# Another spread of filler matmuls over the heads of the recurrent stage of a decoder-layer kernel

## What is computed

```
# mLSTM: 4 heads, 512 prompt tokens (chunkwise in the reference), 8 samples with a state each
s    = (q k^T) * exp(d_log - m_t);  den = w_inter * (q n) + s.sum(-1)
num  = w_inter * (q C) + s v;       h   = num / max(|den|, exp(-m_t))
C_new = a * C + sum_s w k v^T;      n_new = a * n + sum_s w k
h    = layer-normalised per head, * norm_a_g * sigmoid(a_o)
# merge gates, computed from x alone
gates = sigmoid(einsum('btd,de->bte', x, w_merge))       # (544, 2 * 1024)
```

## The kernel before, in words

| place | c | e3 | e2 | e1 | e0 | g | u1 | u2 | u3 | end |
|---|---|---|---|---|---|---|---|---|---|---|
| steps | 16 | 8 | 4 | 4 | 4 | 4 | 3 | 3 | 2 | 8 |

## Time and profile before

### The profile page before, as it was taken

How to read it: one execution, slowest core, us unless ns; L and a number is a source line. 1 busy time by engine, 2 the same in 40 slices (tenths; PEclk the granted TensorE clock), 3 DMA queues, 4 the chain that set the end, 5 groups by cost and what they waited for, 6 DMA issues and landing times.

```text
span 2187.4 us, 34346 instructions
## 1 busy us (share of the span) xinstructions
PE 2112.9 (97%) x13300; PEld 1868.0 (85%) x13300; DVE 1481.9 (68%) x3063; ACT 986.9 (45%) x1763; POOL 922.1 (42%) x608
## 2 busy tenths in 40 slices
PE   9999999987998998999999999999999999999998
PEld 8898988775565996999999999999998877888886
DVE  4334233346776556487989979876648789888886
ACT  2121332233777431333346676676544455445542
POOL 0000332312110001337877767777765555555530
PEclk9999999997999999999999999999999999999999
DMA  4354343346110543327888899999999999999992
GB/s 148 96 192 116 108 124 102 115 174 164 45 41 1 180 149 113 108 69 230 292 269 298 304 340 319 325 381 403 378 324 404 397 394 377 385 393 393 385 361 84
DMA packets 191242, 518.58 MB, mean 237 GB/s; under 512 B 15796, under 2 KB 85544, under 8 KB 186600
## 3 DMA queue, kind: packets, MB, share of 16 engines
q1 hardware_dynamic: 139656, 330.80, 42.8%
q0 software_dynamic: 50848, 184.53, 22.7%
q10 hardware_dynamic: 576, 1.05, 0.1%
HBM read 446.70 MB, written 73.75 MB: 238 GB/s over the span
## 4 chain that ended last, share of the span: by engine, by line
PE 55%; DVE 3%; DMA 1%; ACT 1%; POOL 0%; issue 0%; DVEq 0%
PE ps_e L2515 23%; PE ps_e L2490 8%; PE ps_e L2485 7%; PE ps_e L2484 7%; PE ps_e L2507 3%; PE ps_e L2539 1%; PE ps_e L2545 1%; PE ps_e L2550 1%; PE ps_e L2546 1%; PE ps_e L2473 1%; DMA v_raw<-in_peer_v 1%; DVE row L2880 1%; DVE one_b L2864 0%; DVE one_a L2864 0%; POOL u_lo L2433 0%
## 5 line engine op out<-in xcount | busy, mean ns | idle before, releaser
L2426 POOL DMA_INDIRECT row<-in_peer_v,sparse_idx x160 | 277.6, 1735 | 209.1 <-DVE y L2888 158.5
L2484 PE MATMUL ps_e<-hTh,u_hi 128*128 128x384 f32 x1024 | 347.1, 339 | 0.0
L2485 PE MATMUL ps_e<-hTl,u_hi 128*128 128x384 f32 x1024 | 346.7, 339 | 0.0
L2433 POOL TENSOR_TENSOR u_lo<-u_raw,u_hi 128x1024 fp32r<-128x1024 f32 x128 | 312.7, 2444 | 66.5 <-ACT u_hi L2590 58.9
L2515 PE MATMUL ps_e<-v_hi,w_hi 128*128 128x512 f32 x768 | 242.4, 397 | 3.2 <-DVE v_lo L2908 3.2
L2515 PE MATMUL ps_e<-v_lo,w_hi 128*128 128x512 f32 x768 | 240.9, 394 | 0.0
L2515 PE MATMUL ps_e<-v_hi,w_lo 128*128 128x512 f32 x768 | 240.6, 394 | 0.0
L2908 DVE TENSOR_TENSOR v_lo<-v_raw,v_hi 128x1024 fp32r<-128x1024 f32 x128 | 158.0, 1237 | 90.1 <-ACT v_hi L2629 89.7
L2490 PE MATMUL ps_e<-hTh,u_lo 128*128 128x384 f32 x1024 | 207.8, 345 | 3.9 <-POOL u_lo L2433 3.9
L2629 ACT CAST v_hi<-v_raw 128x1024 fp32r<-128x1024 f32 x128 | 128.2, 1049 | 156.4 <-DMA v_raw<-in_peer_v 156.4
L2880 DVE CUSTOM_DVE_ANT_0 row<-row,ps_e 128x1024 f32<-128x1024 f32 x150 | 178.8, 1213 | 27.4 <-DMA row<-in_peer_u,sparse_idx 25.4
(11 more groups left out here) (539 smaller groups left out, 4558.7 us busy)
## 6 DMA issues: line engine op xcount, KB each, us to landing
u_raw<-in_peer_uT SPq DMA_DIRECT2D x128, 512.0 KB, 5.8
v_raw<-in_peer_v SPq DMA_DIRECT2D x30, 2048.0 KB, 10.2
hidden_gelu<-gelu_out SPq DMA_DIRECT2D x64, 384.0 KB, 6.4
gate_tables<-g_buf SPq DMA_DIRECT2D x48, 512.0 KB, 9.8
e_gate<-gate_tables SPq DMA_DIRECT2D x31, 768.0 KB, 13.0
gelu_in<-hidden_gelu SPq DMA_DIRECT2D x31, 768.0 KB, 12.9
w_raw<-in_w_tiles SPq DMA_DIRECT2D x45, 512.0 KB, 3.6
gw_raw<-in_merge_tiles SPq DMA_DIRECT2D x16, 512.0 KB, 3.8
```

Of the source, the lines that this page charges most:

```text
L2426: pool.indirect_dma_start(out=row[:, :], out_offset=None, in_=io.peer_u if i < U_END else io.peer_v, in_offset=bass.IndirectOffsetOnAxis(a ...
L2433: pool.tensor_tensor(u_lo[n % UB][:, :, :], u_raw[n % UB][:, :, :], u_hi[:, n % UH, :, :].bitcast(F32), ALU.subtract).then_inc(ul_done, 1)
L2484: pe.matmul(ps[:, n % 2, 0:TD], u_hi[:, n % UH, dc, :], hTh[:, dc, :], start=(dc == 0), stop=False)
L2485: pe.matmul(ps[:, n % 2, 0:TD], u_hi[:, n % UH, dc, :], hTl[:, dc, :], start=False, stop=False)
```

## The change

Before, each place had one number for all heads. After, it has one per head:

```diff
     fill_at, filled = {}, 0
+    spread = {"c": (17, 17, 17, 22), "e3": (8, 8, 8, 12), "e2": (4, 4, 4, 8), "e1": (4, 4, 4, 4), "e0": (4, 4, 4, 4),
+              "g": (4, 4, 4, 3), "u1": (3, 3, 3, 0), "u2": (3, 3, 3, 0), "u3": (2, 2, 2, 0), "end": (8, 8, 8, 0)}
     for key, steps in ([("scan", 24), ("cols", 8)] +
-                       [((h, k), n) for h in range(AH)
-                        for k, n in (("c", 16), ("e3", 8), ("e2", 4), ("e1", 4), ("e0", 4), ("g", 4), ("u1", 3), ("u2", 3),
-                                     ("u3", 2), ("end", 8))]):
+                       [((h, k), spread[k][h]) for h in range(AH)
+                        for k in ("c", "e3", "e2", "e1", "e0", "g", "u1", "u2", "u3", "end")]):
         fill_at[key] = (filled, filled + steps)
         filled += steps
     assert filled == 16 * GT
```

## The result

| | before | after |
|---|---|---|
| median, us | 2195.15 (5 executions, 2194.07 to 2195.67) | 2219.91 (5 executions, 2217.20 to 2226.37) |
| the profiled execution, us | 2189.14 | 2226.37 |
| its span, us | 2187.4 | 2224.7 |
| mean granted clock in it | 0.988 | 0.981 |

The ratio of the medians is 1.0113 (95% interval 1.0098 to 1.0128): 24.8 us slower. That is on the side of the forecast and 2 us beyond the end of its range (2218). In five executions of the same program the granted clock was 0.981, 0.982, 0.984, 0.985 and 0.985, with 2226.4, 2221.4, 2219.9, 2217.5 and 2217.2 us: the time goes with the clock, and the profiled execution is the slowest of the five.

What follows compares the result with a forecast made beforehand. The recurrent stage goes at TensorE's pace, its stalls paid in full. 17.6 + 1.9 - 3.0 = +16.5 us: 2205.6 us from the profiled execution, 2210.8 from the median; range 2205 to 2218.

Steps and rivals of the forecast that it cites:

- The unit ends: Recurrent stage: 22 more filler units end inside a call of fill, each stalling TensorE 0.80 us; +17.6 us.
- ScalarE late: Rival: at seven places in e1 and g ScalarE's copy starts late, 0.5 us more each; +3.6 us, chance 0.08.
- not slower: Rival: the added unit ends cost nothing, something else takes the stalls in; -1.1 us, 2193.2 us, chance 0.05.
- The last head's order: Last head: fillers move ahead of the update products, which then take 5.7 us; VectorE's chain starts 3.5 us later.
- the tail: Stage's end: updates ending 3.5 us later less 1.6 from the early table load; net +1.9 us, between +1.1 and +4.5.
- The next stage: Behind the recurrent stage: wc off the path, pages landing some 8 us behind the opening, not 11.1; -3.0 us.
- its cover: Last head's state store: the whole tail still covers it; otherwise it would hold up SyncE's pages 4 to 7; counted at nothing.
- The early load of -1.6 us: Last head: ScalarE's table load runs ahead of the square root, so a 1.73 us delay shrinks to 0.1.
- The clock: Rival: TensorE's pauses bring one 6.8 us stretch at 1.2 GHz in each head; +13.6 us, 2224.4 us, chance 0.06.

Runs made afterwards that it cites:

- the second profile: The changed kernel measured once more, unaltered, with no 17.1 us clock fall in the heads of its profile: 2223.33 us, ratio 1.0123.
- the split of "c": Kernel before, with 8 of the 16 filler steps in each head's first call moved behind the prompt state's products: 2193.66 us, ratio 0.9988.
- the kernel with the full clock there: Kernel before, fillers in c cut in two around the prompt state's products, last head's 56 steps all ahead of its updates: 2196.94 us, ratio 1.0008.

## Why the prediction was wrong at its end, and right in its main term

**The unit ends: right.** The forecast had 28 places, 22 of them new, at 0.80 us, +17.6. The trace has 28 waits, gaps of 0.87 and 0.20, 12.5 us more idle time and the restart besides. Between the stage's start and the first update of the last head the second profile has 196.5 us and before has 171.35, +25.1; 6.1 of it are the fillers moved ahead and at most 1.7 a fall of 3.4 us at 308.4, which leaves 17.3 to 19.0. (Kernels with 2 to 7 places have such a short fall at that point in some profiles too, so it is not counted to the change.) Between the first updates of heads 0, 1 and 2 that profile has 46.6 and 45.65 us, as forecast (45.5 to 46.7). The shift of one, of two and of three heads give 0.72, 0.64 to 0.74 and 0.79 us a place, the last two from executions at before's clock, and the split of "c" 0.6 by the medians and 0.82 by the traces.

**ScalarE late, and "not slower": both refuted.** No gap in e1 or g is longer than the others, and no place is free.

**The last head's order: mechanism right, size a little small, by the clock.** From the first update product to the end of the last update I had 5.7 us. It is 5.74 in the kernel with the full clock there (470.53 to 476.27), but 6.9 in both profiles of the changed kernel (499.18 to 506.12 in the first), where the clock fell 2.2 and 2.0 us into the updates. From the first update to the transposes of line 831 both take 12.8 us; before it was 15.8 with 6.1 us of fillers in it. So the tail cost 3.1 us instead of 1.9; in the kernel with the full clock in its updates it is 11.6 us, which makes 1.9. The difference of 1.2 us goes with a fall of the clock that the forecast did not have (13.7 us long in both profiles, where before has 6.8 behind its updates). The table load went ahead, as taken from the earlier trace rows, and VectorE's chain to line 948's end took 2.87 us (2.89 forecast).

**The next stage: this step failed.** "So **-3.0 us**, between 0 and -4.7": it was +0.7 and +1.6 in the two profiles, counted from the start of the transposes to the first product on pages (20.8 and 21.8 us, before 20.14); with the last head's order alone it was 0.0. The gain was not there, for two reasons.

The larger part is the pages. wc did leave the path, as forecast, but the pages did not come 8 us behind VectorE's first work: they came 10.7 and 11.4 us behind it (before 11.1), 2.7 and 3.4 late. I had taken the 366 GB/s of the earlier trace rows for them, from a stretch in which wc, pages 4 to 7 and pages 8 to 15 were under way together. With bqT and wc out of the way the span up to the first product on pages moved 219 GB/s (303 before). SyncE's four issues alone ran until 526.43, 4.3 us behind VectorE's first work, and TensorE had its pages 6.4 us after that. So an emptier queue did not bring them sooner. My bound of 0 ("the pages land as late as now") held this part to within 0.3 us, my central value did not.

The smaller part is the barrier, and it was in no bound. From the transposes to VectorE's first work it is 10.1 and 10.4 us, before 9.0: 1.1 and 1.4 more. I had written that without its cover "the state store would hold up SyncE's pages 4 to 7", and then that this "is in the bound of 0"; but SyncE must issue them before the barrier can open, so the delay comes on top of the other terms. The cover did go, and not because the store came late against the tail: bqT and wc now leave ahead of it. The idle time ahead of the barrier went from 1.10 to 2.85 and 3.13 us, and is 3.34, 4.01 and 6.66 in three kernels with the same turn of order. Part of it does not count, since the last transposes pass sooner. With the barrier in it the upper bound should have been about +2. By this step the forecast was 3.7 to 4.6 us low.

The early load of -1.6 us was no gain of its own in the kernel before (0.9996, with an interval of 0.9987 to 1.0006), where the DMA chain would have swallowed it. In the changed kernel VectorE waited 1.75 and 2.0 us longer at the barrier than before, which is more than those 1.6, so it is not shown to have gained anything there either: the path to the barrier ran from the last update (506.12) over the store (506.63) and the page issues (517.17), past the square root and the transposes.

**The clock: a rival with a chance of 0.06 that came true in part.** I priced four falls of 6.8 us, one in each head. It was one of 17.1 us, in four of the five profiles with 16 places or more. Its price from the two profiles of the changed kernel: from the stage's start to the first update of the last head they take 203.8 and 196.5 us, 7.3 apart, and both have the short fall of 3.4 us. I had also put the pauses too close, at one "every 3 to 4 us": in the heads they stand 3.6 to 12.4 us apart without the fall, some 6.6 on average, as seven to a head of 46 us would have told. The row from 540 to 560, on which I rested the low chance, has short pauses at full clock, but it is another stage with other products. The Trainium skill (TensorE: Matmul & The Clock Gate, "A second HAM failure mode: psum-queue depth-cycling") describes micro-idles that make the clock swing; by that rule, which no row of before bore out, the runs agree in kind, with one fall in the heads and not a swinging: in the 84 us ahead of the fall in the profile after, none of TensorE's twelve waits on line 993 was over 0.6 us.

The sum by the second profile, without the long fall: 17.6 + 3.1 + 1.6 = 22.3 us, or 23.7 to the first product on pages (231.04 from the stage's start, before 207.31), as the trace has it with the short fall. Over 2194.8 (before at a clock of 0.988) that is 2217.1 to 2218.5, where the fastest executions of the changed kernel lie (2217.2 to 2217.9); with one fall it is 2224.4 to 2225.8, where its slowest do (2225.3 to 2226.4). Against the forecast of +16.5 the measured +24.8 is 8.3 more: by this sum 4.6 are the next stage, 1.2 the tail, and the other 2.5 or so the fall, which a part of the executions has. Without the fall the sum, 22.3, already stands at the upper end of the 12.7 to 22.3 that I had added up.

**What stays open.** Why one execution has the fall and another has not. A fall of 17.1 us stood in the heads in four of the five profiles with 16 places or more and in none of the nine with fewer (one of 3.4 us stood in head 0's updates when head 0 alone was shifted), so it goes with the pauses; whether their number in a head, their spacing, or the updates behind them decide was not told apart. That executions between 2218 and 2225 us have shorter falls is argued from their clocks alone; they have no profile. The widest spreads, 16.8 us with the shift alone and 14.9 with two heads, are twice the price of one fall, and what those slowest executions have is not shown. Shorter falls, of 3.4 to 13.7 us, stand behind the last head's updates or in them in every profile, that of before too. Also, the last stage of the layer takes 4 to 7 us less in the profile of before than in all others, which makes part of the difference between the two profiled executions (37 us) but not between the medians.

## What to carry to other kernels

Where one accumulator bank is reused, let each accumulation end where other matmuls follow at once, and count the ends that lie inside a call, since here, with TensorE the busy engine, every one was paid in full: a shift by a single step per head made some 22 of them. When a step is moved, write down for each queue what now goes ahead of what; a load that is released earlier can overtake the store for which the barrier waits. A late DMA issue ahead of a barrier is a term of its own, not a bound on another. And a rate read where the queues were full is not the rate of a few transfers that start from an empty queue; issue and landing have to be added up for them.

## What the runs showed of the hardware

Pauses of only 0.55 to 0.58 us, 3.6 to 9.5 us apart in the heads, with 32-row products behind them, went with a fall of TensorE to 1.2 GHz for 17.1 us in four of five profiles; the mean granted clock of a whole execution was 0.986 to 0.990 in the 65 executions of the kernel before that were timed beside the experiments, and 0.978 to 0.988 in the 13 with 28 places.

A table load did not wait for the operand of its activation: it ran at 499.16 to 500.44, and the activation followed 8.6 us later, at 509.03.

The last head's state store (1 MB, GpSimd's queue), issued 1.3 us behind the load of bqT on SyncE's queue, let the pages that wait for it go out 14.6 us after its issue; issued 3.2 us ahead of bqT, 6.0 us after.

Pages behind the barrier came no sooner from emptier queues: 10.7 us behind VectorE's first work at 219 GB/s, against 11.1 at 303.
